# State-space scan of a hybrid layer: two tokens per scan step, drives formed by TensorE and read in PSUM

## The reference

```
u, qkv, z, beta, a, gates = split(rms_norm(x) @ w_in)
h[l] = lambda * h[l-1] + B u[l]          (complex, per group and state; h[-1] given per sample, 0 for the prompt)
y[l] = Re(C h[l]) + D u[l]
y_s5 = gelu(y) * sigmoid(gelu(y) @ w_glu + b_glu)
```

## Time and profile before

| what | value |
|---|---|
| runs, us | 2262.66, 2266.91, 2268.35 |
| span of the profiled execution, us | 2264.2 |
| PE busy | 2124.5 us, 94% |
| DVE busy | 1300.7 us, 57% |
| ACT busy | 837.8 us, 37% |
| POOL busy | 390.8 us, 17% |

### The profile page before, as it was taken

How to read it: one execution, slowest core, us unless ns; L and a number is a source line. 1 busy time by engine, 2 the same in 40 slices (tenths; PEclk the granted TensorE clock), 3 DMA queues, 4 the chain that set the end, 5 groups by cost and what they waited for, 6 DMA issues and landing times.

```text
span 2264.2 us, 35863 instructions
## 1 busy us (share of the span) xinstructions
PE 2124.5 (94%) x14204; PEld 2050.7 (91%) x14204; DVE 1300.7 (57%) x1374; ACT 837.8 (37%) x1042; POOL 390.8 (17%) x373
## 2 busy tenths in 40 slices
PE   4887887799999999999999999999999999999998
PEld 3876776699899999789999999999999999999997
DVE  4699999986645443877444444433344444444553
ACT  4433232256523232253444333333333333333543
POOL 3844545610000010310110000000000000000110
PEclk9998888899999999999999999999999999999999
DMA  5622322245323345677544444544444444444452
GB/s 126 186 84 66 102 75 84 81 144 148 100 83 111 86 125 148 189 221 241 164 148 149 148 148 148 154 139 150 148 152 150 150 150 149 139 152 150 143 156 89
DMA packets 298894, 309.98 MB, mean 137 GB/s; under 512 B 24674, under 2 KB 289971, under 8 KB 297843
## 3 DMA queue, kind: packets, MB, share of 16 engines
q1 hardware_dynamic: 279648, 291.87, 42.2%
q0 software_dynamic: 3264, 11.64, 2.0%
q10 hardware_dynamic: 15878, 5.02, 1.1%
HBM read 291.34 MB, written 17.14 MB: 136 GB/s over the span
## 4 chain that ended last, share of the span: by engine, by line
PE 75%; DVE 17%; issue 3%; ACT 2%; ACTq 1%; DMA 1%; SPq 0%; DVEq 0%
PE pg L1900 67%; DVE wlo L1268 4%; PE side_a L1925 3%; DVE gg L1424 2%; DVE tt L1444 2%; DVE tt L1424 2%; PE side_b L1925 2%; DVE bu L1424 2%; DVE cacc L1549 1%; DVE bu L1429 1%; DVE gg L1452 1%; DMA raw<-in_w_out 0%; ACTq L938 0%; PE side_a L1900 0%; ACT whi L845 0%
## 5 line engine op out<-in xcount | busy, mean ns | idle before, releaser
L1268 DVE TENSOR_TENSOR wlo<-raw,whi 128x1024 fp32r<-128x1024 f32 (+1 forms) x528 | 664.5, 1267 | 712.1 <-ACT whi L845 709.6
L845 ACT ACTIVATE whi<-raw 128x1024 fp32r<-128x1024 f32 (+1 forms) x528 | 545.0, 1039 | 1017.3 <-PE pg L1900 974.5
L1900 PE MATMUL pg<-xhi,whi 128*128 128x320 f32 x2816 | 894.1, 318 | 7.6 <-DVE wlo L1268 7.6
L1900 PE MATMUL pg<-xlo,whi 128*128 128x320 f32 x2816 | 881.9, 313 | 0.0
L1900 PE MATMUL pg<-xhi,wlo 128*128 128x320 f32 x2816 | 881.0, 313 | 0.0
L1900 PEld LDWEIGHTS pg<-xhi,whi 128*128 128x128 f32 x2816 | 540.3, 192 | 33.3 <-issue 26.6
L1900 PEld LDWEIGHTS pg<-xlo,whi 128*128 128x128 f32 x2816 | 540.2, 192 | 0.8
L1900 PEld LDWEIGHTS pg<-xhi,wlo 128*128 128x128 f32 x2816 | 539.2, 191 | 0.0
L1900 PE MATMUL pg<-mhi,whi 128*128 128x320 f32 x704 | 217.6, 309 | 2.5 <-DVE wlo L1268 2.5
L1900 PE MATMUL pg<-mhi,wlo 128*128 128x320 f32 x704 | 217.5, 309 | 0.0
L1900 PE MATMUL pg<-mlo,whi 128*128 128x320 f32 x704 | 217.5, 309 | 0.0
(11 more groups left out here) (421 smaller groups left out, 2347.4 us busy)
## 6 DMA issues: line engine op xcount, KB each, us to landing
raw<-in_w_in SPq DMA_DIRECT2D x144, 512.0 KB, 3.7
raw<-in_w_gate SPq DMA_DIRECT2D x88, 512.0 KB, 3.5
raw<-in_w_up SPq DMA_DIRECT2D x88, 512.0 KB, 3.5
raw<-in_w_down SPq DMA_DIRECT2D x80, 512.0 KB, 3.6
raw<-in_w_out SPq DMA_DIRECT2D x32, 512.0 KB, 3.6
raw<-in_w_ple_gate SPq DMA_DIRECT2D x32, 512.0 KB, 3.6
raw<-in_w_a SPq DMA_DIRECT2D x16, 512.0 KB, 5.3
raw<-in_w_b SPq DMA_DIRECT2D x16, 512.0 KB, 4.5
```

The source lines that it names most:

```text
L845: act.activation(whi[:, r, 0:nk, :], raw[:, r, 0:nk, :], ACT.Copy).then_inc(w_hi, 1)
L1268: dve.tensor_tensor(wlo[:, r, 0:nk, :], raw[:, r, 0:nk, :], whi[:, r, 0:nk, :].bitcast(F32), ALU.subtract).then_inc(w_lo, 1)
L1900: ins = pe.matmul(out[:, m, 0:N], w, a, start=first and k == 0 and part == 0, stop=last and k == nk - 1 and part == 2)
```

## The change

The scan runs over chunks of Q = 2 tokens: 160 columns (NCK) instead of 320. With b = B and lambda b = (lambda B), the drive of a chunk is (lambda B) u[even] + B u[odd], summed by TensorE in PSUM, and the scan steps with lambda squared. The scan yields the state after each odd token, from which the odd outputs are read. An even output is read from the state before it: Re(C lambda h[prev]) + k0 u[even], with k0 = Re(C B). `yt` is stored with even and odd tokens apart.

- VectorE's operations of a slot have 320 elements instead of 640 and the four drive products read PSUM; the copy to `bu` on ScalarE goes. The sample's starting terms are added after the rotation.
- `drive` becomes 8 matmuls of 160 columns into one region. `readout` becomes 13: one with `k0`, 4 with `ct` (160 columns), 4 with `ctl` (127), and 4 of 32 columns that read the samples' previous states from `hs`, which ScalarE writes in `last_states`.
- GpSimd's phases have 256 elements. One of its tables has one doubling fewer, and two squares are added.
- Built before the slots: `b_discrete` forms B and lambda B (12 operations, 8 spreads), `bb` transposes four groups of 8, `k0` is formed by 64 small matmuls, and `c_advanced` forms C lambda on VectorE (12 operations of 512) at the end of `ba`.
- The `glu` product and the u results are written through a view that reorders even and odd tokens.

The diff, cut to its core:

```
+Q = 2
+NCK = N // Q
+PCK, SCK = NPR // Q, NL // Q
...
-    slot([("ba",)], 4)
+    slot([("k0",), ("ba",)], 4)
...
-        order += [("a", ("bu", hq, 0)), ("b", ("bu", hq, 1))]
+        order += [("b", ("bu", hq))]
...
# ScalarE, slot s5
-                    for t in range(2):
-                        wait_filled(act, ("bu", hq, t))
-                        drain(copy(bu[:, :, t, :], ps(("bu", hq, t))[:, :, 0:N]), ("bu", hq, t))
...
# ScalarE, last_states
+                o.step(copy(hs[:, s, :, :, :, 0], h0s[:, :, tiles, :]))
+                src = gg[:, s, :, :, PCK:NCK].rearrange("p r t (b l) -> p (r t) b l", l=SCK)[:, :, :, 0:SCK - 1]
+                copy(hs[:, s].rearrange("p r t b l -> p (r t) b l")[:, :, :, 1:SCK], src).then_inc(sem("before_ready"), 1)
...
# VectorE, b_discrete
+                product(bt, bnat, cr, ci)
+                spread(bt, 1)
+                product(bnat, bt, lr, li)
+                spread(bnat, 0)
...
+            def c_advanced():
+                wait_filled(dve, ("k0",))
+                for k in range(2):
...
+                    o.step(dve.tensor_tensor(v(ctl, 0), v(ct, 0), lr, ALU.mult))
+                    o.link(dve.tensor_tensor(tmp, v(ct, 1), li, ALU.mult))
+                    o.step(dve.tensor_tensor(v(ctl, 0), v(ctl, 0), tmp, ALU.add))
...
# VectorE, s5_tiles
-                br, bi, tr, ti = bu[:, 0], bu[:, 1], tt[:, 0], tt[:, 1]
+                tr, ti, tx = tt[:, 0], tt[:, 1], tt[:, 2]
+                drive = ps(("bu", hq))
+                br, bi = drive[:, :, 0:NCK], drive[:, :, NCK:2 * NCK]
...
-                op(br, ui, br, ALU.mult, 2)
-                op(gr_, tr, ti, ALU.add, 2)
-                op(gi, gi, br, ALU.subtract, 1)
+                drain(dve.tensor_tensor(tx, ui, br, ALU.mult), ("bu", hq))
+                op(gr_, tr, ti, ALU.add, 1)
+                wait_drained(dve, ("bu", hq))
+                op(gi, gi, tx, ALU.subtract, 1)
+                starts = gg[:, s, :, :, PCK:NCK:SCK]
+                op(starts, starts, a0[:, :, 2 * hq:2 * hq + 2, :], ALU.add, 0)
...
# TensorE, side k0
+                    for k in range(K5):
+                        for r in range(2):
+                            for q in range(4):
+                                lhs = bmix[:, r, 1, 4 * k + q].rearrange("p h c -> p (h c)")
+                                ins = pe.matmul(out[32 * q:32 * q + 32, 0, 32 * k:32 * k + 32], lhs,
+                                                ct[:, r, k, 32 * q:32 * q + 32], start=r == 0, stop=r == 1)
...
# TensorE, drive
+                for r in range(2):
+                    for j in range(Q):
+                        for t in range(2):
...
+                            ins = pe.matmul(out[:, t, r * NCK:(r + 1) * NCK], bbt[rows, r, j, c, :], yt[rows, c, j, :],
+                                            start=j == 0, stop=j == Q - 1)
...
# TensorE, readout
+                pe.matmul(out[rows, 0, 0:NCK], k0[rows, c, :], yt[rows, c, 0, :], start=True, stop=False)
+                for r in range(2):
+                    for t in range(2):
...
+                        pe.matmul(out[o32, 1, 0:NCK], ct[:, r, c, o32], gg[:, s, r, t, :], start=r == 0, stop=r == 1)
+                        pe.matmul(out[o32, 0, 1:PCK], ctl[:, r, c, o32], gg[:, s, r, t, 0:PCK - 1], start=False, stop=False)
+                pe.wait_ge(sem("before_ready"), hq + 1)
...
+                        ins = pe.matmul(out[o32, 0, PCK:NCK], ctl[:, r, c, o32], hs[:, s, r, t].rearrange("p b l -> p (b l)"),
+                                        start=False, stop=r == 1)
```

More of the change, by code:

```diff
@@ L344, in hybrid_layer @@
         bnat = zpar.take("bnat", [P, 2, NT, 16])
+        h0n = Zone(nc, zpar.end, 2048).take("h0n", [P, 2, 2, P])
+        zpre3 = Zone(nc, ct_end - 3 * 2048, 3 * 2048)
+        bt = zpre3.take("bt", [P, 2, NT, 16])
+        btmp = zpre3.take("btmp", [P, NT, 16])
+        hlo = Zone(nc, arena_at + 16384, 3072).take("hlo", [P, 2, 3, P])
         zba = Zone(nc, arena_at - 3 * N * 4, 3 * N * 4)
@@ L657, in powers @@
                 w = sc5w
-                cur = (sr, si)
-                for k in range(1, 5):
-                    nxt = (w[:, 2 * (k % 2), :], w[:, 2 * (k % 2) + 1, :])
+                cur, n = (sr, si), 2
+                while True:
+                    k = n.bit_length() % 2
+                    nxt = (w[:, 2 * k, :], w[:, 2 * k + 1, :])
                     square(nxt[0], nxt[1], cur[0], cur[1], [w[:, 4 + e, :] for e in range(3)])
                     cur = nxt
[L663 to L669, removed]
@@ L672, in tables @@
+                    n *= 2
             def tables():
                 wait_drained(pool, ("s5par",))
-                cur = powers(tb, sp5[:, 1, :], sp5[:, 2, :])
-                powers(ta, *cur)
+                w = [sc5w[:, k, :] for k in range(12)]
+                square(w[8], w[9], sp5[:, 1, :], sp5[:, 2, :], w[4:7])
+                square(w[10], w[11], sp5[:, 3, :], sp5[:, 4, :], w[4:7])
+                cur = powers(tb, 16, w[8], w[9])
+                o.step(pool.tensor_copy(w[8], cur[0]))
@@ L1406, in b_discrete @@
[L1406 to L1411, removed]
+                lr = sp5[:, 3, :].unsqueeze(2).broadcast_to([P, NT, 16])
@@ L1426, in s5_tiles @@
                 dve.wait_ge(sem("phases_ready"), hq + 1)
[L1427 to L1429 removed]
+                wait_filled(dve, ("bu", hq))
+                o.settle()
                 op(tr, ur, br, ALU.mult)
@@ L1527, in side @@
                     dve.wait_ge(sem("pads_done"), 1)
+                    c_advanced()
                 elif what == "s5":
@@ L2152, in drive @@
                 pe.wait_ge(evacuated, hq // 4 + 1)
-                for t in range(2):
-                    key = ("bu", hq, t)
-                    c, q = (2 * hq + t) // 4, (2 * hq + t) % 4
-                    rows = slice(32 * q, 32 * q + 32)
-                    out = begin(key)
-                    for r in range(2):
-                        ins = pe.matmul(out[:, r, 0:N], bbt[rows, r, c, :], yt[rows, c, :], start=True, stop=True)
-                    end(ins, key)
+                if hq == 0:
+                    for j in range(Q):
+                        wait_drained(pe, ("bbt", 1, j))
@@ new lines, in drive @@
+                key = ("bu", hq)
+                out = begin(key)
+                for r in range(2):
+                    for j in range(Q):
+                        for t in range(2):
+                            c, q = (2 * hq + t) // 4, (2 * hq + t) % 4
+                            rows = slice(32 * q, 32 * q + 32)
+                            ins = pe.matmul(out[:, t, r * NCK:(r + 1) * NCK], bbt[rows, r, j, c, :], yt[rows, c, j, :],
+                                            start=j == 0, stop=j == Q - 1)
@@ L2162, in readout @@
+                end(ins, key)
             def readout(hq):
                 key = ("y", hq)
+                s, c, rows = hq % 2, hq // 2, slice(64 * (hq % 2), 64 * (hq % 2) + 64)
                 pe.wait_ge(sem("states_ready"), hq + 1)
                 if hq == 0:
-                    wait_drained(pe, ("ct", 1))
+                    wait_drained(pe, ("k0",))
+                    pe.wait_ge(sem("ctl_ready"), 2)
                 out = begin(key)
-                for t in range(2):
-                    c, q = (2 * hq + t) // 4, (2 * hq + t) % 4
-                    for r in range(2):
-                        ins = pe.matmul(out[32 * q:32 * q + 32, 0, 0:N], ct[:, r, c, 32 * q:32 * q + 32], gg[:, hq % 2, r, t, :],
-                                        start=r == 0, stop=r == 1)
+                pe.matmul(out[rows, 0, 0:NCK], k0[rows, c, :], yt[rows, c, 0, :], start=True, stop=False)
```

183 lines of the change are left out of this document (116 added, 67 removed).

## The result

The changed kernel takes 2174.5 us (median of 4 runs, 2173.6 to 2176.1) against 2265.4 us for the kernel before in the same comparison (4 runs, 2262.7 to 2268.4). The ratio is 0.9600, with a 95% interval from 0.9586 to 0.9614. The span of the profiled execution is 2174.4 us, for 2264.2 before. The prediction was 2182 us, with 2172 to 2197 as the forecast's own range. The time of a run lies 1.7 to 1.9 us above the span of the same run; the 2.7 us given with the time before compares a median with the span of another execution.

What follows compares the result with a forecast made beforehand. VectorE was taken to bound the slots. First drive 130.1 plus units, drives, readouts and 4 us put the last readout at 382.5, 84.7 us earlier: span 2179.5, plus 2.7, 2182 us; own range 2172 to 2197, 8-in-10 range 2165 to 2215.

Steps and rivals of the forecast that it cites:

- the 110 us of waits and low clock: TensorE's loss from first drive to last readout before: 347.9 us less 238 of work, the most a cheaper VectorE can give.
- VectorE in a slot: VectorE's slot operations take 7.4 us; with wlo, pair results and GpSimd's disturbance 14.9 us a slot, for 22.3 before.
- by 0.4 us only: In the slots TensorE, at 15.3 us, becomes the bound just above VectorE at 14.9 us.
- GpSimd against VectorE: In the slots GpSimd's phases take 6.4 us, stretched, and VectorE loses 2.8 us a slot to them.
- TensorE in a slot: Units 3.44 x 3.52 us, a drive 1.3 and a readout 1.9 us: 15.3 us a slot.
- allowance of 4 us: Given in all for TensorE's waits in the slots, including 0.2 us for before_ready in every second slot and the first slots.
- Before the slots: Preparation: b_discrete ends at 85.4, units start at 91.2, k0 takes 6 us, c_advanced is just covered, first drive at 130.1.
- The rules weighed: Two skill rules: PSUM sources would lengthen VectorE's slot 0.26 us; tiling drains would bring readouts nearer 2.4 us, time 8 us longer.
- VectorE as the bound: Rival for the slots: VectorE stays the bound at 17.4 us a slot, time 2210 us; chance 0.2.
- Full overlap and small preparation: Rival for readouts and preparation: readout 1.4 us, k0 3.5 us, no waits, time 2168 us; chance 0.14.
- The low clock: Rival: TensorE's units stay at the low clock, 7.04 us each, a slot 30.6 us, time 2422 us; chance 0.02.
- The bare preparation: Rival before the slots: k0 takes 14 us and c_advanced's 8 us are not covered, time 2198 us; chance 0.07.

Runs made afterwards that it cites:

- three kernels: The kernel before without GpSimd's phase products from slot 2 on (2203.5 us), with VectorE's slot operations on one of two tiles (2200.1 us), and with both edits (2198.2 us).
- both reliefs: The kernel before without GpSimd's phase products from slot 2 on and with VectorE's slot operations on one of two tiles: 2198.2 us.
- the two kernels that show it: The kernel before with both edits that relieve VectorE, 2198.2 us; the changed kernel with drives in the readouts' region, copied out by ScalarE, 2210.9 us.
- the run with region a: The changed kernel with drives filled into side_a, the readouts' region, and copied to SBUF by ScalarE: 2210.9 us.
- the run with B first: The changed kernel with TensorE transposing B before lambda B, while VectorE still forms lambda B: 2176.4 us.

## Why the prediction was right

**The time.** Predicted 2182 us, measured 2174.5, 7.7 us less. Of that the first drive is 1.7 us (128.4 for 130.1), the slots 0.9 (251.5 for 252.4), what follows them 2.5 (1794.5 for 1797.0) and the step from span to median 2.6 (0.1 for 2.7). That these are small is in part luck, as the next paragraphs show: terms in them were off by more and cancelled.

**What bounded the kernel before.** Half right. VectorE was the bound, and 64 to 69 us come from relieving it alone (three kernels). But the prediction put all of the 110 us of waits and low clock down to a dear VectorE. Parted by the end of the last readout, the gain is this:

| step | measured | from |
|---|---|---|
| VectorE's bound | -70.1 us | first drive to last readout: 347.9 before, 277.8 (120.2 to 398.0) with both reliefs |
| the wait for the drive's copy | -26.3 us | 277.8 against 251.5 in the kernel after |
| first drive later | +9.1 us | 119.3 to 128.4 |
| after the slots | -2.5 us | 1797.0 to 1794.5, within the scatter |
| sum | -89.8 us | 2264.2 to 2174.4 |

The second row is net of the readouts, 27.7 us in all for 16 x 1.21 = 19.4 at the full clock before, so the wait itself was worth some 35 us, as in the two kernels that show it. A sign of it stood in the trace before, in the waits of 140 to 449 us:

```profile
PE side_a L2172 <- ACT bu L848: 36.1, 14, 4.2
ACT hl L848 <- DVE gg L1452: 34.5, 8, 10.0
PE side_a L2159 <- DVE yt L1459: 30.3, 8, 4.3
```

But the first row isn't the copy's alone. ScalarE keeps the last states (`hl`) ahead of the copy, and in 8 of these slots it had itself waited for VectorE's states, so that VectorE stands behind those waits; in the others it came from a weight split, as above. How the two share the 36 us only the relieved kernels told. The prediction did name the copies, but as ScalarE's busy time ("nothing, it is 28% busy"); as what PE waited for it didn't price them. The total came out because it was built from what PE needs after the change, where both waits are gone, and not from the waits that it removes. Had the drives been copied out of the readout's region as before, the same reasoning would have been wrong by some 35 us (the run with region a).

**VectorE in a slot.** Right: operations of 320 elements came 0.40 us apart, a scan took 0.81 us with 1.52 us for two, the starting terms 0.22 us, and a PSUM source cost no more. The sum for a slot was too high all the same: 14.9 us forecast, 12.7 measured (183.5 us busy in 224, at 15.5 us a slot). The forecast that PE becomes the bound "by 0.4 us only" was thus too cautious; measured is a slack of 2.3 us, in which four added products of 2.1 us found room and twelve did not.

**GpSimd against VectorE.** This is the term that was off. GpSimd works 4 x 1.21 + 2 x 0.98 + 0.31 = 7.1 us a slot where 6.4 was forecast, but VectorE loses 0.7 us a slot by it (183.5 against 172.8 us) and not 2.8. The forecast took over the rate of loss of one slot before, and the drive products, which now read PSUM, lose nothing (last section). `wlo` is 1.42 us in the mean, for 1.22 undisturbed.

**TensorE in a slot.** Predicted 252.4 us from first drive to last readout (382.5 - 130.1), measured 251.5. The parts differ: the drives take 16 x 1.29 = 20.6 (20.8 forecast), the sixteen readouts 27.7 in all (30.4; the wait for `before_ready` in every second slot came as 0.16 us for 0.2), and the units 203.2 (197 and 4 of allowance). No unit waited. So the allowance of 4 us, given for waits, covered something else. The surplus is a start: behind a drive or a readout a run of n units takes 3.52 n + 0.19 us (3.71, 7.23, 10.76 and 14.27 us in the chain), and 31 such runs are 5.9 us. The row 108.59 of the earlier trace rows has 10.79 for 3 x 3.52 = 10.56 already.

**Before the slots.** First drive at 130.1 forecast, 128.4 measured, by two errors that nearly cancel. `b_discrete` ended at 85.6 (85.4). Then PE, which had stood idle for 3.4 us, ran its transposes at 1.97, 1.71 and 1.72 us a group, with the granted clock at 0.69 in this stretch, where the run with B first shows 1.06 us a group at 1.00:

```profile
84.00:95.00 11.00, 9.18 (x55) 8.87 (x56) 9.80 (x11) 4.10 (x4) 4.01 (x7) 0.69 0.45 133
```

So the units started at 94.25 and not at 91.2. The prediction had paced these groups by ScalarE's copies of 1.01 us alone. Against it, `k0` took 1.2 us where the forecast said 6 and its lower bound 3.5:

```profile
L2054 PE MATMUL side_a<-ct,bmix x128: 196/196/217, 108.3 to 109.4; 128*32 128x32 f32 x128
```

(duration in ns, least, median and most; first and last start). The 64 matmuls are 128 records, 10 ns apart, so they overlap. The bound had been taken from matmuls with 128 weight columns and scaled by weights. These have 32 weight columns and go to four column groups in turn; whether that is why they are so fast no run isolates. `c_advanced` ran on VectorE from 123.0 to 131.2, and the first `wlo` of slot 0 started at 131.97; PE's units and drives behind 117.65 show no wait, so it was covered as forecast.

**The rules weighed.** The extra cycles for a PSUM source, of the Trainium skill's "VectorE: DVE Perf Modes", section "The TRN2 errata", don't show: a product with its drive in PSUM takes 478 ns, those that read SBUF alone 472 to 493. The 0.26 us that the prediction worked out by that rule for four products of a slot aren't there. The drain at a change of tiling mode, of the Trainium skill's "TensorEngine Tiling (Array Packing)", section "Key Properties", agrees with the 0.19 us at the start of each run of units behind a drive or a readout; behind transposes of the units' own tiling, 128 rows and 128 columns, four units take 14.08 us = 4 x 3.52 and there is no such start (row 94.25). What of the 0.19 us is a drain no run here tells. The readout with its additional change took 1.66 to 1.82 us and didn't reach 2.4.

**The rivals.** VectorE as the bound (0.2) failed by 2.3 us of slack a slot. With operations 0.5 us apart and 1.3 us of waits, as it supposed, 2.5 us, all of that would have been gone. Full overlap and small preparation (0.14) was right on `k0` and half right on the readout. The low clock (0.02) appeared nowhere in the slots, as PE never stood. The bare preparation (0.07) failed on both of its terms, `k0` and `c_advanced`.

## What to carry to other kernels

Predict a stage from what the next bound needs, and then list every wait of that engine in the old trace with its releaser: those that the change doesn't touch remain. A wait's releaser may itself have waited: follow it one step further before you give the wait a cause. A PSUM region that a product and its consumer's result share is a wait, if the engine that empties it has work ahead of it in its queue that waits for the first engine; relieving the busiest engine first shows it. Before you sum gains, try each alone: here two edits were worth 64 and 67 us, and together 69.

## What the hardware showed unexpectedly

- **A small fp32 matmul costs far less than its record lasts**: 64 of them, with 128x32 weights, 32 columns and four column groups in turn, took 1.3 us, 20 ns each, though one record lasts 196 ns.
- **A PSUM source spares VectorE the disturbance by GpSimd.** Two records of GpSimd (POOL) and a drive product of VectorE beside them, first in the kernel after, then with the drives copied to SBUF:

```profile
158.66 2.06 POOL L594 TENSOR_TENSOR pt<-ta,tb 128x256 f32<-128x256 f32 x2
159.59 0.87 DVE L1490 TENSOR_TENSOR tt<-uu,side_b 128x320 f32<-128x320 f32 x2
```

```profile
158.91 2.31 POOL L595 TENSOR_TENSOR pt<-ta,tb 128x256 f32<-128x256 f32 x2
159.84 0.90 DVE L1493 TENSOR_TENSOR tt<-uu,bur 128x320 f32<-128x320 f32 x1
```

  Two products from PSUM take 0.87 us, one from SBUF 0.90. None of the 60 drive products from PSUM at 140 to 380 us took more than 0.482 us. VectorE's busy time in 140 to 364 us rose from 183.5 to 196.2 us by the copy, at no cost in time, as there was slack.
